# A hybrid decoder layer on one core: the chunk inverse of the delta rule, packed into two 64x64 quarters of the array

## The chip, the core and the metric

The kernel runs on one core of a Trainium2 chip. Its engines are TensorE (PE in the profile; its weight loads are the row PEld), VectorE (DVE), ScalarE (ACT), GpSimd (POOL) and SyncE (SP), which issues most transfers. Each engine takes its own instructions in order and waits on semaphores that others raise. The metric is the device time of one execution in microseconds; less is better.

## The reference, cut to what matters

One layer of a decoder: a norm, one input projection, three groups of heads (sparse attention, Mamba-2, gated DeltaNet), an output projection and an MLP. The change touches the gated DeltaNet scan alone. Per chunk and head it does this:

```python
decay = jnp.exp(jnp.where(incl, cum[..., :, None] - cum[..., None, :], -jnp.inf))
kk = jnp.einsum('bhik,bhjk->bhij', kc, kc)
lower = eye + jnp.where(strict, kk * decay, 0.0) * bc[..., :, None]
rhs = vc * bc[..., None] - jnp.einsum('bhik,bhkv->bhiv', kc * (bc * jnp.exp(cum))[..., None], Sf)
u = lax.linalg.triangular_solve(lower, rhs, left_side=True, lower=True, unit_diagonal=True)
```

`lower` is a unit lower triangular matrix per head, and there are 6 heads of width 128. Everything is float32.

## The kernel before, in words

The work runs in stages: input projection with the sample attention beside it, causal convolutions (`convolve`), the chunk scans (`scans`), the scans' tail, gates and norms, attention with the output projection, and the MLP. Barriers stand between `scans` and its neighbours, so what it saves or loses moves all that follows.

`scans` takes four chunks of 128 tokens (i = 0 to 3) and a tail of 48 tokens (i = 4). Two programs run interleaved on every engine, and `turns()` is the written order in which they alternate. `states()` carries the recurrent states of Mamba-2 ("ssd") and DeltaNet ("gdn") from chunk to chunk. `inverses()` has no recurrence and makes for each chunk the transposed inverse `ttT` of the 6 matrices, one chunk ahead of its use.

`inverses()` for a chunk: PE transposes keys and queries (L1187) and spreads the gates (L1190); DVE and ACT make the decay; PE multiplies keys by keys and queries (L1199); DVE forms the strictly upper triangle `lT` (L1443) and the attention matrix `atT` (L1448). Then the inverse is doubled level by level, from blocks of 1 to blocks of 128: seven levels for a whole chunk, four for the tail. A level k does, for two sets of three heads (x = 0 and 1, one PSUM bank `a_ps[x]` and one `c_ps[x]` each):

- POOL: `mT` = `lT` times a 0/1 mask of the level (L1328), up to two levels ahead, into a ring of two
- PE: `a_ps` = `mT`ᵀ `t` (L1211); ACT copies it into `p1` (L1268)
- PE: `a_ps` = `ttT`ᵀ `p1` (L1217, not at the last level) and `c_ps` = `p1`ᵀ `ttT` (L1220)
- DVE: `ttT` -= `c_ps` (L1467) and `t` -= `a_ps` (L1470)

Level 0 is only identity minus mask: L1457 and L1460. All products are 128x128x128 (48x48x48 in the tail), and a float32 product shows as two records on PE and two on PEld. Lines of `states()` that the text names: L1126 and L1130 (ssd: spread gates, B by C), L1347 (DVE: their differences), L1136, L1363 (DVE: decay by B·C), L1145 and L1149 (ssd: products with the inputs), L1157 (gdn: keys and queries by the state), L1388 to L1398 (DVE: what follows it), L1298 (POOL: `wk`). The turns of a chunk, by PE: L1187, L1190 | state | L1199 | state | level 0, level 1 | state | level 2 | state | level 3 | state | level 4, level 5 | state | level 6. The fourth chunk has fewer state turns.

Of the kernel before, what the change touches and what calls it, by code (L numbers as in the profile page):

```python
# [16 lines left out]
P = 128  # L17
# [1036 lines left out]

def scans(nc, dram, consts, sb):


    with ExitStack() as ctx:
# [24 lines left out]
        mT = lambda k: mT_ring[:, k % 2]  # L1083
# [5 lines left out]
                   "rows_done", "dif", "dec_ready", "decU_ready", "products", "lt_ready", "at_ready", "m_ready")  # L1089
# [7 lines left out]
        lev0 = lambda i: 7 * i  # L1097
        product_ps = lambda c: (a_ps[0], a_ps[1], c_ps[0])[c]
        block = ctx.enter_context(nc.Block())

        @block.sync
        def _(sp):
            sp.dma_start(level[0][:, :], consts["c_level"]).then_inc(p["level_in"], 16)
            sp.dma_start(level[1][:, :], consts["c_level_tail"]).then_inc(p["level_in"], 16)
            sp.wait_ge(p["level_in"], 32)

        @block.tensor
        def _(pe):
# [68 lines left out]
            def inverses():  # L1177
                yield
                for i in range(5):
# [23 lines left out]
                    for lev in range(nlev(i)):  # L1203
                        k = lev0(i) + lev
                        pe.wait_ge(p["m_ready"], k + 1)
                        for x, hs in sets:
                            if lev:
                                pe.wait_ge(t_ready[x], k)
                            for h in range(hs.start, hs.stop):
                                rhs = t[0:n, h, 0:n] if lev else ident[0:n, 0:n]  # L1210
                                last = pe.matmul(a_ps[x][0:n, h % 3, 0:n], mT(k)[0:n, h, 0:n], rhs, start=True, stop=True)  # L1211
                            last.then_inc(p1_done[x], 1)
                        for x, hs in sets if lev else ():
                            pe.wait_ge(p1_out[x], p1_count(i, lev))
                            if lev < nlev(i) - 1:
                                for h in range(hs.start, hs.stop):
                                    pe.matmul(a_ps[x][0:n, h % 3, 0:n], ttT(i)[0:n, h, 0:n], p1[0:n, h, 0:n],  # L1217
                                              start=True, stop=True)
                            for h in range(hs.start, hs.stop):
                                last = pe.matmul(c_ps[x][0:n, h % 3, 0:n], p1[0:n, h, 0:n], ttT(i)[0:n, h, 0:n],  # L1220
                                                 start=True, stop=True)
# [8 lines left out]
        def _(act):  # L1230
# [19 lines left out]
            def inverses():  # L1250
                yield
                for i in range(5):
# [8 lines left out]
                    yield  # L1261
                    yield
                    yield
                    for lev in range(1, nlev(i)):
                        k = lev0(i) + lev
                        for x, hs in sets:
                            act.wait_ge(p1_done[x], k + 1)
                            act.activation(p1[0:n, hs, 0:n], a_ps[x][0:n, 0:3, 0:n], ACT.Copy).then_inc(p1_out[x], 1)  # L1268
# [5 lines left out]
        def _(pool):  # L1274
# [29 lines left out]
            def inverses():  # L1304
                pool.wait_ge(p["level_in"], 32)
                yield
                for i in range(5):
# [12 lines left out]
                    for lev in range(nlev(i)):  # L1320
                        k = lev0(i) + lev
                        for x, _ in sets:
                            if k >= 2:
                                pool.wait_ge(p1_done[x], k - 1)
                            if lev == 2:
                                pool.wait_ge(t_ready[x], k - 1)
                        mask = level[i == 4][0:n, P * lev:P * lev + n]
                        pool.tensor_tensor(mT(k)[0:n, :, 0:n], lT[0:n, :, 0:n], bc(mask.unsqueeze(1), [n, HC, n]), ALU.mult  # L1328
                                           ).then_inc(p["m_ready"], 1)
# [5 lines left out]
        def _(dve):  # L1335
# [83 lines left out]
            def inverses():  # L1419
                yield  # L1420
                scaled_inputs(0)
                for i in range(5):
# [16 lines left out]
                    if i:  # L1439
                        dve.wait_ge(p["m_ready"], lev0(i))  # L1440
# [10 lines left out]
                    yield  # L1451
                    for lev in range(nlev(i)):
                        k = lev0(i) + lev
# [2745 lines left out]
```

## Time and profile before

| | |
|---|---|
| median of 3 runs | 3156.24 us |
| lowest and highest | 3148.05 and 3164.49 us |
| span of the profiled execution | 3150.1 us |
| mean granted clock of TensorE over the span | 0.962 |
| PE busy | 2957.6 us, 94% |
| the four chunks and the tail in `scans`, masks on | 1099.3 to 1332 us |

No device time of the profiled execution stands apart from its span, which lies inside the range of the runs. Times in the rows are microseconds from the span's start. A granted clock of 1.00 is TensorE's 2.4 GHz, 0.50 its 1.2 GHz, and a value between is a share of time at each. "128*128 128x384" is the weights' shape and then what streams; "idle before" in brackets is how long the engine stood and what ended it.

### The profile page before, as it was taken

The page shows a single profiled execution, that of the slowest core. Times are in us where ns is not written, and L with a number is a line of the kernel's source. Part 1 is how long each engine was busy: PE and PEld are TensorE (multiplying, and loading weights), DVE is VectorE, ACT ScalarE, POOL GpSimd, SP SyncE. Part 2 cuts the span into 40 slices and gives each one's busy share as a digit, 9 for nine tenths or more (in the row PEclk, how much of TensorE's full clock was granted, in tenths as well). Part 3 has the DMA queues.
Part 4 walks back from the last instruction along what each step waited for, and adds up shares of the span by engine and source line. Part 5 has one row for each costly group of instructions (what it writes and reads, how often), then busy time and mean ns, then how long its engine had stood idle before and what let it go on. Part 6 is the DMA issues. An engine that isn't in the chain of part 4 may idle for free. (4 is left out here: it accounts for less than half of the span.)

```text
span 3150.1 us, 51111 instructions
## 1 busy us (share of the span) xinstructions
PE 2957.6 (94%) x20787; PEld 2752.5 (87%) x20787; DVE 2360.1 (75%) x3067; ACT 1181.0 (37%) x1736; POOL 667.5 (21%) x477
## 2 busy tenths in 40 slices
PE   7999999999996588887999899999999999999998
PEld 6987898999875487746888899999999999999998
DVE  6149985799543666557985789888988888888887
ACT  4232221222454411134324455555555333333332
POOL 4442333567251143334340000000000000000000
PEclk9999999999997699888999999999999999999999
DMA  5442333569684000048433466666667955565552
GB/s 185 116 141 82 92 102 90 155 214 281 207 256 156 25 1 1 14 128 227 130 108 133 129 187 201 192 184 199 189 194 212 352 180 181 190 205 178 190 171 104
DMA packets 503689, 494.76 MB, mean 157 GB/s; under 512 B 33738, under 2 KB 440618, under 8 KB 501941
## 3 DMA queue, kind: packets, MB, share of 16 engines
q1 hardware_dynamic: 467312, 421.23, 43.9%
q0 software_dynamic: 12928, 42.02, 4.3%
q10 hardware_dynamic: 23216, 28.24, 2.6%
q8 instruction: 166, 2.72, 0.4%
q14 instruction: 67, 0.55, 0.1%
HBM read 378.49 MB, written 114.12 MB: 156 GB/s over the span
## 5 line engine op out<-in xcount | busy, mean ns | idle before, releaser
L3726 PE MATMUL om_ps<-om_hc,om_ring 128*128 128x272 f32 x5376 | 683.3, 290 | 10.6 <-DVE om_ring L3775 6.4
L3726 PEld LDWEIGHTS om_ps<-om_hc,om_ring 128*128 128x128 f32 x5376 | 682.3, 189 | 11.7 <-DVE om_ring L3775 6.8
L3743 PE MATMUL om_ps<-om_hc,om_ring 128*128 128x272 f32 x5376 | 680.8, 290 | 6.6 <-issue 5.1
L3743 PEld LDWEIGHTS om_ps<-om_hc,om_ring 128*128 128x128 f32 x5376 | 679.8, 189 | 7.5 <-issue 6.7
L3962 ACT ACTIVATE om_ring<-om_late 128x1024 fp32r<-128x1024 f32 x301 | 318.7, 1059 | 385.1 <-PE om_ps L3743 263.0
L3775 DVE TENSOR_TENSOR om_ring<-om_late,om_ring 128x1024 fp32r<-128x1024 f32 x301 | 366.1, 1221 | 79.2 <-ACT om_ring L3962 79.0
L565 PE MATMUL pm_ps<-h,w_ring 128*128 128x280 f32 x2688 | 354.9, 293 | 8.4 <-issue 7.8
L565 PEld LDWEIGHTS pm_ps<-h,w_ring 128*128 128x128 f32 x2688 | 348.7, 189 | 14.3 <-issue 14.2
L504 POOL TENSOR_TENSOR w_ring<-w_raw,w_ring 128x1024 fp32r<-128x1024 f32 (+2 forms) x106 | 244.5, 2327 | 340.6 <-ACT w_ring L600 340.4
L3962 ACT ACTIVATE om_ring<-om_raw 128x1024 fp32r<-128x1024 f32 x155 | 164.1, 1059 | 203.2 <-PE om_ps L3743 124.2
L583 PE MATMUL pm_ps<-w_ring,h 128*128 128x512 f32 (+2 forms) x1152 | 237.3, 365 | 2.7 <-PEq L2764 2.7
L583 PEld LDWEIGHTS pm_ps<-w_ring,h 128*128 128x128 f32 x1152 | 199.8, 189 | 36.8 <-issue 3.0
L3775 DVE TENSOR_TENSOR om_ring<-om_raw,om_ring 128x1024 fp32r<-128x1024 f32 x155 | 188.8, 1221 | 50.2 <-ACT om_ring L3962 50.2
L600 ACT ACTIVATE w_ring<-w_raw 128x1024 fp32r<-128x1024 f32 (+2 forms) x124 | 120.8, 1009 | 273.9 <-PE as_dead_bank L583 187.4
L3893 DVE TENSOR_TENSOR om_x<-om_x,om_ps 128x544 f32<-128x544 f32 x224 | 160.6, 717 | 79.0 <-PE om_ps L3743 76.8
L2269 PE MATMUL ao_w<-ao_mh,ao_ring 128*128 128x272 f32 x1152 | 180.0, 308 | 2.2 <-DVE ao_mh L2460 2.2
L2269 PEld LDWEIGHTS ao_w<-ao_mh,ao_ring 128*128 128x128 f32 x1152 | 155.8, 192 | 18.6 <-issue 12.5
L632 ACT ACTIVATE pm_stage<-pm_ps 128x280 f32<-128x280 f32 (+3 forms) x64 | 29.1, 455 | 179.0 <-PE pm_ps L565 133.7
L3278 DVE TENSOR_TENSOR as_prod<-as_rows,as_qb 128x512 f32<-128x512 f32 x64 | 95.7, 1495 | 0.0
L3159 POOL DMA_INDIRECT as_rows<-in_cache_v,as_offs x64 | 71.8, 1122 | 89.1 <-PE as_o_bank L3425 75.0
L565 PEld LDWEIGHTS pi_ps<-h,w_ring 128*128 128x128 f32 x672 | 86.4, 188 | 0.9 <-issue 0.8
L565 PE MATMUL pi_ps<-h,w_ring 128*128 128x280 f32 x672 | 86.9, 291 | 0.0
(614 smaller groups left out, 4111.6 us busy)
## 6 DMA issues: line engine op xcount, KB each, us to landing
hid_scratch<-om_x SPq DMA_DIRECT2D x64, 952.0 KB, 7.4
om_hc<-hid_scratch SPq DMA_DIRECT2D x56, 1088.0 KB, 11.7
w_raw<-in_w_in SPq DMA_DIRECT2D x112, 512.0 KB, 4.2
om_late<-in_w_up SPq DMA_DIRECT2D x85, 512.0 KB, 5.0
om_late<-in_w_down SPq DMA_DIRECT2D x85, 512.0 KB, 5.2
om_raw<-in_w_up SPq DMA_DIRECT2D x43, 512.0 KB, 4.8
om_raw<-in_w_down SPq DMA_DIRECT2D x43, 512.0 KB, 5.0
ao_raw<-in_w_out SPq DMA_DIRECT2D x32, 384.0 KB, 3.9
```

Source lines behind the costliest of these rows:

```text
L504: eng.tensor_tensor(f32r(ring[:, n % 2, 1, half_of(q, n)]), raw[:, q, whole(q, n)], ring[:, n % 2, 0, half_of(q, n)], ALU.subtract).then_i ...
L565: ins = pe.matmul(bank_of(b + y)[:, 0:HALF], piece(a, k), f32r(h[:, x, k, two_halves(y)]), start=first, stop=last)
L583: ins = pe.matmul(bank_of(b + m)[:, 0:w], f32r(h[:, x, ld.k0 + k, tok]), piece(a, k), start=first, stop=last)
L600: act.activation(f32r(ring[:, n % 2, 0, half_of(q, n)]), raw[:, q, whole(q, n)], ACT.Copy).then_inc(hi_ready[q], 1)
L2269: ins = pe.matmul(w_ps[2 * (n % 2) + half][:, 0:HM], w, f32r(mh[:, b, k, kept_half(half)]), start=first, stop=last)
L3159: pool.indirect_dma_start(self.rows[:, n % RING, :], None, table, bass.IndirectOffsetOnAxis(ap=self.offs[:, x, j:j + 1], axis=0)).then_inc ...
L3278: dve.tensor_tensor(prod[:, n % 2, :], self.rows[:, n % RING, :], self.qb[:, j % 4, :], ALU.mult).then_inc(s["multiplied"], 1)
L3726: last = pe.matmul(ps[:, bank_of(q, idx), 0:HM], f32r(ring[:, n % SLOTS, a, P * k:P * (k + 1)]), f32r(hc[:, c, b, k, :]), start=(idx in (0 ...
L3743: last = pe.matmul(ps[:, bank_of(q, idx) + i, 0:HM], w, f32r(hc[:, slot, b, GJ * half + j, :]), start=(idx in (0, 1, 3) and j == a == b == 0),
L3775: dve.tensor_tensor(f32r(ring[:, n % SLOTS, 1, :]), source(n), ring[:, n % SLOTS, 0, :], ALU.subtract).then_inc(lo, 1)
L3893: dve.tensor_tensor(dst, dst, ps[:, b:b + 2, 0:HM], ALU.add).then_inc(gathered, 1)
L3962: act.activation(f32r(ring[:, n % SLOTS, 0, :]), source(n), ACT.Copy).then_inc(hi, 1)
```

## The change

For whole chunks the first six levels, in which all is block diagonal with two blocks of 64, keep only the two blocks, one above the other: `t`, `p1`, the new `tt` and `lp`, and the masks' ring hold 64 columns a head in place of 128. A product of 128x128x128 becomes two of 64x64x64, one with both operands and its result in partitions 0 to 63, one in 64 to 127, issued in turn into the same bank. The last level is one off-diagonal block: two products of 64x64x64 a head, and DVE writes it negated. ACT makes a packed copy `lp` of `lT` from which POOL takes the masks of levels 1 to 5; level 0 takes them from `lT` in two halves; the mask of level 6 is gone. The tail keeps its shapes. The level table is loaded as 6x64 columns in two transfers. Buffers shrink with it, and an `eye` and two zeroed blocks are written once.

```diff
+HB2 = P // 2
+PACKED = 6
+BLOCKS = (slice(0, HB2), slice(HB2, P))
...
-        level = [sbuf("level", [P, 7 * P]), sbuf("level_tail", [P, 4 * P])]
-        lT, t, p1, dec, decU, beta_upto = (sbuf(n, [P, HC, P]) for n in ("lT", "t", "p1", "dec", "decU", "beta_upto"))
-        mT_ring = sbuf("mT", [P, 2, HC, P])
+        level, level_tail = sbuf("level", [P, PACKED, HB2]), sbuf("level_tail", [P, 4 * P])
+        lT, dec, decU, beta_upto = (sbuf(n, [P, HC, P]) for n in ("lT", "dec", "decU", "beta_upto"))
+        lp, t, p1, tt = (sbuf(n, [P, HC, HB2]) for n in ("lp", "t", "p1", "tt"))
+        mT_ring = sbuf("mT", [P, 2, HC, HB2])
...
                             for h in range(hs.start, hs.stop):
-                                rhs = t[0:n, h, 0:n] if lev else ident[0:n, 0:n]
-                                last = pe.matmul(a_ps[x][0:n, h % 3, 0:n], mT(k)[0:n, h, 0:n], rhs, start=True, stop=True)
+                                if join:
+                                    last = pe.matmul(a_ps[x][BLOCKS[1], h % 3, 0:HB2], lT[BLOCKS[0], h, BLOCKS[1]],
+                                                     t[BLOCKS[0], h, :], start=True, stop=True)
+                                    continue
+                                for b in blocks_of(i):
+                                    w = b.stop - b.start
+                                    rhs = t[b, h, 0:w] if lev else eye[b, 0:w]
+                                    last = pe.matmul(a_ps[x][b, h % 3, 0:w], mT(m)[b, h, 0:w], rhs, start=True, stop=True)
...
                                 for h in range(hs.start, hs.stop):
-                                    pe.matmul(a_ps[x][0:n, h % 3, 0:n], ttT(i)[0:n, h, 0:n], p1[0:n, h, 0:n],
-                                              start=True, stop=True)
+                                    for b in blocks_of(i)[0:1] if lev == PACKED - 1 else blocks_of(i):
+                                        w = b.stop - b.start
+                                        pe.matmul(a_ps[x][b, h % 3, 0:w], tt[b, h, 0:w], p1[b, h, 0:w], start=True, stop=True)
...
+                    if i < 4:
+                        act.wait_ge(p["lt_ready"], i + 1)
+                        if i:
+                            act.wait_ge(p["m_ready"], masks_before(i))
+                        for b in BLOCKS:
+                            act.activation(lp[b, :, :], lT[b, :, b], ACT.Copy).then_inc(p["lp_ready"], 1)
...
-                            act.activation(p1[0:n, hs, 0:n], a_ps[x][0:n, 0:3, 0:n], ACT.Copy).then_inc(p1_out[x], 1)
+                            act.activation(p1[b, hs, 0:w], a_ps[x][b, 0:3, 0:w], ACT.Copy).then_inc(p1_out[x], 1)
...
+                        elif lev == 0:
+                            for b in BLOCKS:
+                                last = pool.tensor_tensor(mT(m)[b, :, :], lT[b, :, b],
+                                                          bc(level[b, lev, :].unsqueeze(1), [HB2, HC, HB2]), ALU.mult)
+                            last.then_inc(p["m_ready"], 1)
+                            pool.wait_ge(p["m_ready"], m + 1)
+                        else:
+                            pool.wait_ge(p["lp_ready"], 2 * (i + 1))
+                            pool.tensor_tensor(mT(m), lp[:, :, :], bc(level[:, lev, :].unsqueeze(1), [P, HC, HB2]), ALU.mult
+                                               ).then_inc(p["m_ready"], 1)
...
+                            if i < 4 and lev == PACKED:
+                                last = dve.tensor_scalar(ttT(i)[BLOCKS[0], hs, BLOCKS[1]], c_ps[x][BLOCKS[0], 0:3, 0:HB2], -1.0,
+                                                         None, ALU.mult)
+                            elif i < 4 and lev == PACKED - 1:
+                                for b in BLOCKS:
+                                    dve.tensor_tensor(ttT(i)[b, hs, b], tt[b, hs, :], c_ps[x][b, 0:3, 0:HB2], ALU.subtract)
+                                b = BLOCKS[0]
+                                last = dve.tensor_tensor(t[b, hs, :], t[b, hs, :], a_ps[x][b, 0:3, 0:HB2], ALU.subtract)
...
+                            else:
+                                dve.tensor_tensor(tt[0:n, hs, 0:w], tt[0:n, hs, 0:w], c_ps[x][0:n, 0:3, 0:w], ALU.subtract)
+                                last = dve.tensor_tensor(t[0:n, hs, 0:w], t[0:n, hs, 0:w], a_ps[x][0:n, 0:3, 0:w],
                                                          ALU.subtract)
```

The order on PE, from level 5 of the first chunk to the transposes of the second. First before (columns: line, operation, result and operands, shape, count):

```order
L1211 MATMUL sc_a<-sc_t,sc_mT 128x128 x6
L1217 MATMUL sc_a<-sc_p,sc_ttT 128x128 x3
L1220 MATMUL sc_c<-sc_ttT,sc_p 128x128 x3
L1217 MATMUL sc_a<-sc_p,sc_ttT 128x128 x3
L1220 MATMUL sc_c<-sc_ttT,sc_p 128x128 x3
L1157 MATMUL sc_e<-st,sc_kq 128x128 x12
L1211 MATMUL sc_a<-sc_t,sc_mT 128x128 x6
L1220 MATMUL sc_c<-sc_ttT,sc_p 128x128 x6
L1187 MATMUL sc_a<-ident,tm 128x128 x12
```

Then the same place in the changed kernel:

```order
L1240 MATMUL sc_a<-sc_t,sc_mT 64x64 x12
L1254 MATMUL sc_a<-sc_p,sc_tt 64x64 x3
L1258 MATMUL sc_c<-sc_tt,sc_p 64x64 x6
L1254 MATMUL sc_a<-sc_p,sc_tt 64x64 x3
L1258 MATMUL sc_c<-sc_tt,sc_p 64x64 x6
L1176 MATMUL sc_e<-st,sc_kq 128x128 x12
L1234 MATMUL sc_a<-sc_t,sc_lT 64x64 x6
L1246 MATMUL sc_c<-sc_ttT,sc_p 64x64 x6
L1206 MATMUL sc_a<-ident,tm 128x128 x12
```

Nothing has changed places: each group of three heads is twice as many products of an eighth of the size each, the product into `a_ps` at level 5 is made for the upper block alone, and level 6 has one product a head in each of its two steps.

On GpSimd the masks of a chunk, before (the second chunk, from `decU` on):

```order
L1316 TENSOR_TENSOR sc_decU<-sc_dec,sc_beta_upto 128x768
L1328 TENSOR_TENSOR sc_mT<-sc_lT,sc_level 128x768
L1328 TENSOR_TENSOR sc_mT<-sc_lT,sc_level 128x768
L1283 TENSOR_TENSOR sc_xdt<-tm,dt 128x768
L1285 TENSOR_TENSOR sc_skip<-tm,ssm_d 128x768
```

and in the changed kernel:

```order
L1362 TENSOR_TENSOR sc_decU<-sc_dec,sc_beta_upto 128x768
L1382 TENSOR_TENSOR sc_mT<-sc_lT,sc_level 64x384
L1382 TENSOR_TENSOR sc_mT<-sc_lT,sc_level 64x384
L1388 TENSOR_TENSOR sc_mT<-sc_lp,sc_level 128x384
L1329 TENSOR_TENSOR sc_xdt<-tm,dt 128x768
```

The mask of level 0 has become two operations of half the partitions and half the columns, and that of level 1 one of half the columns, which waits for ACT's copy.

## Rows read from the trace of the kernel before

**Rows 1.** The page: busy time, share of the span and instructions of each engine.

```profile
PE 2957.6 (94%) x20787; PEld 2752.5 (87%) x20787; DVE 2360.1 (75%) x3067; ACT 1181.0 (37%) x1736; POOL 667.5 (21%) x477
```

**Rows 2.** Windows: stretch, length, PE, PEld, DVE, ACT, POOL busy, PEclk, DMA, GB/s.

```profile
1217.50:1275.50 58.00, 50.50 (x374) 45.75 (x373) 38.01 (x75) 10.12 (x19) 22.95 (x13) 0.94 0.00 1
```

**Rows 3.** Timeline of one inverse level with no other work between.

```profile
1302.71 0.91 PE L1211 MATMUL sc_a<-sc_t,sc_mT 128*128 128x128 f32 x6
...
1303.66 0.49 ACT L1268 ACTIVATE sc_p<-sc_a 128x384 f32<-128x384 f32 x1 [3.03 <-PE sc_a L1211]
...
1304.73 0.83 PE L1217 MATMUL sc_a<-sc_p,sc_ttT 128*128 128x128 f32 x6
...
1305.40 0.83 PE L1220 MATMUL sc_c<-sc_ttT,sc_p 128*128 128x128 f32 x6
...
1306.35 0.56 DVE L1467 TENSOR_TENSOR sc_ttT<-sc_ttT,sc_c 128x384 f32<-128x384 f32 x1 [2.44 <-PE sc_c L1220]
...
1307.51 0.68 PE L1211 MATMUL sc_a<-sc_t,sc_mT 128*128 128x128 f32 x4
```

**Rows 4.** Timeline of the third chunk: what its queues wait for.

```profile
1219.48 1.57 PE L1211 MATMUL sc_a<-ident,sc_mT 128*128 128x128 f32 x12 [0.49 <-POOL sc_mT L1328]
1220.21 1.72 DVE L1457 TENSOR_TENSOR sc_ttT<-ident,sc_mT 128x768 f32<-128x768 f32 x1
...
1222.66 1.57 PE L1211 MATMUL sc_a<-sc_t,sc_mT 128*128 128x128 f32 x12 [1.60 <-DVE sc_t L1460]
...
1226.93 2.84 PE L1126 MATMUL sc_e<-upto,g 128*128 128x128 f32 x24
...
1238.06 3.90 DVE L1363 TENSOR_TENSOR sc_sdec<-sc_sdec,sc_gm 128x768 f32<-128x768 f32 x2
...
1242.22 3.38 PE L1145 MATMUL sc_e<-sc_xdt,sc_sdec 128*128 128x64 f32 x24 [2.32 <-DVE sc_sdec L1363]
...
1247.94 1.50 PE L1211 MATMUL sc_a<-sc_t,sc_mT 128*128 128x128 f32 x12
...
1252.23 0.91 PE L1211 MATMUL sc_a<-sc_t,sc_mT 128*128 128x128 f32 x6
...
1256.93 2.84 PE L1157 MATMUL sc_e<-st,sc_kq 128*128 128x128 f32 x24
...
1264.78 3.50 PE L1187 MATMUL sc_a<-ident,tm 128*128 128x128 f32 x12 [2.15 <-DVE sc_ttT L1467]
```

**Rows 5.** Timeline: L1363 in the first chunk, GpSimd idle.

```profile
1094.10 2.17 DVE L1363 TENSOR_TENSOR sc_sdec<-sc_sdec,sc_gm 128x768 f32<-128x768 f32 x2 [1.26 <-ACT sc_sdec L1236]
```

**Rows 6.** Timeline of the tail: products of 48x48, and a change of size.

```profile
1319.00 1.63 PEld L1170 LDWEIGHTS sc_e<-sc_u,sc_wk 128*128 128x128 f32 x12 [0.25 <-issue]
...
1325.13 0.35 PEld L1220 LDWEIGHTS sc_c<-ttT_tail,sc_p 48*48 48x48 f32 x6
...
1327.09 0.28 ACT L1268 ACTIVATE sc_p<-sc_a 48x144 f32<-48x144 f32 x1 [2.00 <-PE sc_a L1211]
...
1328.73 0.29 DVE L1467 TENSOR_TENSOR ttT_tail<-ttT_tail,sc_c 48x144 f32<-48x144 f32 x1 [1.96 <-PE sc_c L1220]
...
1388.30 1.39 PEld L1669 LDWEIGHTS tl_e<-tl_xdt,tl_sdec 48*48 48x48 f32 x24 [0.21 <-issue]
```

**Rows 7.** GpSimd's masks, by tile sc_lT: minimum/median/maximum ns.

```profile
L1328 POOL TENSOR_TENSOR sc_mT<-sc_lT,sc_level x28: 1796/1813/2238, 1099.3 to 1300.2; 128x768 f32<-128x768 f32 x28
L1328 POOL TENSOR_TENSOR sc_mT<-sc_lT,sc_level_tail x4: 786/794/805, 1319.8 to 1325.0; 48x288 f32<-48x288 f32 x4
```

**Rows 8.** The same columns as rows 2, in stretches of two us.

```profile
1245.50:1247.50 2.00, 2.00 (x5) 1.09 (x5) 1.23 (x3) 0.00 (x0) 0.00 (x0) 0.50 0.00 0
1324.00:1326.00 2.00, 1.84 (x36) 1.74 (x36) 0.41 (x3) 0.55 (x2) 1.54 (x2) 1.00 0.00 0
1328.00:1330.00 2.00, 2.00 (x26) 1.90 (x24) 0.82 (x4) 0.00 (x0) 0.00 (x0) 0.50 0.00 0
1376.00:1378.00 2.00, 2.00 (x7) 0.74 (x6) 0.09 (x1) 1.86 (x2) 0.05 (x1) 1.00 0.90 343
```

More of the change, by code:

```diff
@@ L1102, in _ @@
         def _(sp):
[L1103 to L1105 removed]
+            by_level = consts["c_level"].rearrange("p (l c) -> p l c", c=P)
+            for b in BLOCKS:
+                sp.dma_start(level[b, :, :], by_level[b, 0:PACKED, b]).then_inc(p["level_in"], 16)
+            sp.dma_start(level_tail[:, :], consts["c_level_tail"]).then_inc(p["level_in"], 16)
+            sp.wait_ge(p["level_in"], 48)
         @block.tensor
@@ L1203, in inverses @@
                     for lev in range(nlev(i)):
-                        k = lev0(i) + lev
-                        pe.wait_ge(p["m_ready"], k + 1)
+                        k, m = lev0(i) + lev, masks_before(i) + lev
+                        join = i < 4 and lev == PACKED
+                        if not join:
+                            pe.wait_ge(p["m_ready"], m + 1)
+                        if k == 0:
+                            pe.wait_ge(p["eye_ready"], 2)
                         for x, hs in sets:
@@ L1214, in inverses @@
                             pe.wait_ge(p1_out[x], p1_count(i, lev))
+                            if join:
+                                for h in range(hs.start, hs.stop):
+                                    last = pe.matmul(c_ps[x][BLOCKS[0], h % 3, 0:HB2], p1[BLOCKS[1], h, :],
+                                                     ttT(i)[BLOCKS[1], h, BLOCKS[1]], start=True, stop=True)
+                                last.then_inc(q_done[x], 1)
+                                continue
                             if lev < nlev(i) - 1:
                                 for h in range(hs.start, hs.stop):
-                                    pe.matmul(a_ps[x][0:n, h % 3, 0:n], ttT(i)[0:n, h, 0:n], p1[0:n, h, 0:n],
-                                              start=True, stop=True)
+                                    for b in blocks_of(i)[0:1] if lev == PACKED - 1 else blocks_of(i):
+                                        w = b.stop - b.start
+                                        pe.matmul(a_ps[x][b, h % 3, 0:w], tt[b, h, 0:w], p1[b, h, 0:w], start=True, stop=True)
                             for h in range(hs.start, hs.stop):
-                                last = pe.matmul(c_ps[x][0:n, h % 3, 0:n], p1[0:n, h, 0:n], ttT(i)[0:n, h, 0:n],
-                                                 start=True, stop=True)
+                                for b in blocks_of(i):
+                                    w = b.stop - b.start
+                                    last = pe.matmul(c_ps[x][b, h % 3, 0:w], p1[b, h, 0:w], tt[b, h, 0:w],
+                                                     start=True, stop=True)
                             last.then_inc(q_done[x], 1)
@@ L1304, in inverses @@
             def inverses():
[L1305 removed]
+                pool.wait_ge(p["level_in"], 48)
                 yield
@@ L1419, in inverses @@
             def inverses():
+                for b in BLOCKS:
+                    dve.tensor_copy(eye[b, :], sb["ident"][b, b]).then_inc(p["eye_ready"], 1)
+                for n in range(2):
+                    dve.memset(ttT_ring[BLOCKS[1], n, :, BLOCKS[0]], 0.0).then_inc(p["eye_ready"], 1)
+                dve.wait_ge(p["eye_ready"], 4)
                 yield
@@ L1439, in inverses @@
                     if i:
-                        dve.wait_ge(p["m_ready"], lev0(i))
+                        dve.wait_ge(p["m_ready"], masks_before(i))
+                        dve.wait_ge(p["lp_ready"], 2 * i)
+                        for x, _ in sets:
+                            dve.wait_ge(p1_done[x], lev0(i))
                     for c in range(3):
```

47 lines of the change are left out of this document (30 added, 17 removed).

## Prediction

> **What bounds the kernel now.** I read the page first: PE is busy for 94% of the span [rows 1], but the change touches only the scans, so the stretch decides and not the share. The windows cut the scans into periods. From one chunk's level 0 to the next it is 58 us, with PE busy for 50.5, DVE for 38.0, ACT for 10.1 and GpSimd for 23.0, at a mean granted clock of 0.94 [rows 2]. The timeline of a period says which wait ends last where [rows 4]. PE waits four times: for the mask of level 0 (0.49 us), for DVE's first `t` (1.60), for DVE's decay products L1363 before L1145 (2.32), and for DVE's last `ttT` before the transposes (2.15). Between these it runs without a gap. So the period is a chain that passes from PE to DVE and back, and a faster PE alone gains only where PE carries it.
>
> A level with nothing between shows the chain itself [rows 3]: 4.80 us from L1211 to L1211. The first group of three heads is 6 records; its end is seen by ACT 0.95 us after its start (1302.71 to 1303.66), ACT copies in 0.49, two further groups a set take 0.67 each (L1217 at 1304.73, L1220 at 1305.40), DVE starts 0.28 after the latter and PE 1.16 after DVE. A group of 6 records passes in 0.67 us, 111 ns a record.
>
> **The change, part by part.**
>
> *PE's products.* A group of 6 records becomes 12 of 64 columns. The nearest row for one: 24 records of 48 weights and 64 streamed columns in the tail of the scans take 1.39 us, 57 ns each, all in one quarter [rows 6]. If the two quarters do not overlap, a group is 12 x 57 = 0.68 us against 0.67: nothing gained. If they overlap fully, 0.34. No row shows two quarters at work at once, so both ends stay open. The fastest issue that a row shows is no help: six loads of 48 columns within 0.35 us, under 58 ns each, and 2 x 48 columns at 2.4 GHz are 40 of these, the stream and not the issue [rows 6]. I take 0.35 for a group in the overlapped case.
> The Trainium skill ("TensorE: Matmul & The Clock Gate", Part 3) states that products in different row and column tiles run side by side with starts some 4 ns apart; by it the group costs 0.34 us. No row here shows it.
>
> *DVE and ACT.* 384 columns cost DVE 0.55 to 0.56 us and 144 cost 0.29; ACT 0.49 and 0.28 [rows 3, 6]. For 192 columns I take 0.35 and 0.32. That is 0.2 less for each of four DVE operations a level and 0.17 for a copy on the chain. L1457 at level 0, 1.72 us for 768 columns, halves to 0.86. Level 5 has three DVE operations a set in place of two and stays even; level 6 is 0.35 against 0.55.
>
> *GpSimd.* 288 columns take 0.79 us, 768 take 1.81 [rows 7]; 384 then take 1.0. Level 0 needs two of them, 2.0 against 1.81, and PE waits for this mask: 0.2 lost a chunk. The others are halved and lie under PE's levels. L1363 takes 3.90 us in the third chunk, where `wk` (L1298) runs on GpSimd beside it [rows 4], and 2.17 in the first, with GpSimd idle [rows 5]. In the changed order `wk` stands in the same place but starts when level 3's first product ends, so its overlap may shrink or not: 0 to 1.7 us gained, and I take 0.3.
>
> *Costed at nothing.* ACT's two `lp` copies (64x384, about 0.5 each by the 0.49 for 384 columns) start when `lT` is ready; ACT's next work is level 1's `p1`, some 6 us later, and the level 1 mask that waits for them is issued behind 2.0 us of level 0 masks. Without that cover they would cost 1.0 a chunk. The `eye` copies, the zero writes (under 1.5 us together at 0.35 each) and the narrower level table (128 x 6 pieces of 256 bytes) come before the first mask by 15 us or more and are under the scan's first gates.
>
> *Change of size.* Behind products of 48 weight columns, PE stands 0.25 us before the first full-width load of L1170 [rows 6]. A chunk now has ten such changes, five blocks of small products. Three lie on the chain (level 1 to L1126, L1149 to level 4, level 5 to L1157); 3 x 0.2 = 0.6 a chunk.
> "TensorEngine Tiling (Array Packing)", Key Properties, in the Trainium skill says that changing the mode drains the engine; the row agrees with a drain of about this size.
>
> *The sum if quarters overlap and the clock stays.* Third chunk, from [rows 4]: level 0, from 1219.48 to 1222.66: 0.86 and 0.2 less on DVE, 1.06. Level 1, 1222.66 to 1226.93 = 4.27, becomes 0.35 + 0.3 + 0.32 + 0.25 + 4 x 0.35 = 2.6: 1.6. Level 2 falls under DVE's queue, which now leads: four updates x 0.2 = 0.8, and L1363 0.3. Level 4: 4.8 becomes (0.35 + 0.3 + 0.32 + 0.3 + 0.7 + 0.28 + 0.76) = 3.0; in this chunk it was 4.3 (1247.94 to 1252.23), since both sets were ready, so 1.3. Level 5, 1252.23 to 1256.93 = 4.7, becomes 2.6: 2.1. Level 6 is hidden under DVE's four us of L1388 to L1398; its two updates give 0.4. Less 0.2 for the mask and 0.6 for the changes of size: 1.06 + 1.6 + 0.8 + 0.3 + 1.3 + 2.1 + 0.4 - 0.8 = 6.8. Three such periods: 20. The fourth chunk has four levels of 4.4 to 4.8 in a row or nearly: 1.1 at level 0, 1.5 at each of levels 1, 4 and 5, 1.3 + 0.4 around levels 2 and 3, 2.2 at level 6, less 0.6: about 9. Together 29 us.
>
> *The clock.* This is where I choose against that sum. In the tail, whose products are all 48x48, the granted clock is 1.00 at 1324 and 0.50 at 1328 to 1330, though PE is busy for all of those two us [rows 8]. In the chunks it fell to 0.50 only after PE had stood (1245.5, behind the wait for L1363) [rows 8]. Yet weights of 48 columns streaming 384 columns held 1.00 at 1376, with PE busy throughout [rows 8]. The packed levels lie between: 64x64, two at once, with PE standing longer for DVE than now (4 to 5 us before L1145). So part of the levels should run at 1.2 GHz. There an overlapped group costs 6 x 111 = 0.67, as now, and the full-width work behind it is slower until the clock returns: L1126 and L1130 (3.1 us) and L1157 (2.7) could each double, and L1145 lose 1. If all of it is at half clock, a chunk keeps the 1.06 of level 0, 0.3 for each of levels 4 and 5, about 0.4 at level 2 and 0.4 at level 6, less 0.8: 1.7 gained against 6.8 lost, 5 slower; three of these and nothing in the fourth make 15 us. I take the middle of 29 gained and 15 lost, 7 to 10 gained, as neither end has a row that decides: 9.
> The same first page of the skill, Part 1, says that the clock follows how busy the engine is; by it the sum of 29 would stand. The tail's row disagrees.
>
> The sum is made on an execution of 3150.1 us span, 0.2% below the median, and is taken from the median: 3156.2 - 9 = 3147.
>
> **The rivals.**
>
> *Overlap at full clock:* the 29 us, less if a record pair takes nearer 90 ns than 58 (then about 20). 3126 to 3137, middle 3130. For it: the row at 1376. Against: the rows at 1328.
>
> *No overlap, full clock:* both quarters write one bank, `a_ps[x]` or `c_ps[x]`; if their results or loads queue, PE's group stays at 0.68. What is left is level 0 (1.06), 0.2 at level 2, 0.9 at level 5 (its `a_ps` product is half), 0.4 at level 6, less 0.2 and 0.6 to 0.8: 1.8 a chunk, three times, and 4 in the fourth, where level 6's 24 records replace 24 of twice the length: 9 to 10 gained. 3147. It would give my time for another reason.
> The skill's "TensorEngine Tiling (Array Packing)", Gotcha 1, says that different row tiles cannot use one PSUM bank at the same time; by it this is the case.
>
> *Slower, the clock:* overlap, but nearly every level and what follows at 1.2 GHz: 15 lost, 3171. It decides against the change from the point where 29/44, two thirds, of this part of the scans are at half clock.
>
> *Slower, both:* no overlap and half clock: 72 records of 111 ns are 8.0 us a level against 4.0; four levels, 1.3 at level 0 and 2.7 at level 5 make 20 a chunk, 15 to 20 of it uncovered, and the 6.8 above: 85 to 105 us, 3250.
>
> **How the numbers follow.** Part of the levels at half clock, my forecast, 0.35, from 3136 to 3160. Overlap at full clock 0.27. No overlap at full clock 0.13. Nearly all at half clock 0.13. Both 0.08. The remaining 0.04 is a cost that I do not see. A difference within 0.5%, 15.8 us, is about what a measurement of this kernel cannot tell from no change. Faster by more than that, under 3140.5: nearly all of the second case and a quarter of the first, 0.33. Slower, over 3172: the last two and under half of the fourth, 0.19. Within: 0.48. The range leaves out the last two cases and the far end of the second: 3124 to 3172.
>
> **What would show it.** After: a level with nothing between of 3.0 us, a group of 12 weight loads within 0.35 to 0.4 us (overlap) or 0.68 (none); PE standing 4 us or more before L1164, as L1145 is then called; the granted clock of a chunk's period 0.7 to 0.85 (my case), 0.9 or more (the fast one), 0.6 (the slow one); periods of 51 (fast), 55 to 57 (mine) or over 60 us. The prediction is wrong if the clock holds, or if the quarters queue and the clock falls.

## The result and the profile after

The changed kernel takes 3117.19 us (median of 4 runs, 3116.68 to 3122.01), the kernel before on the same chip 3152.88. The ratio is 0.9889 with a 95% interval of 0.9861 to 0.9917: 1.1% faster, 36 us by the medians. The prediction was 3147, with a range of 3124 to 3172. The result lies below the range; the gain is nearer to the 29 us that the prediction had summed and then discounted than to the 9 that it forecast.

The page of the profiled execution (span 3115.0 us), the line that answers to [rows 1]:

```profile
PE 2917.8 (94%) x21507; PEld 2709.4 (87%) x21507; DVE 2337.9 (75%) x3079; ACT 1178.1 (38%) x1744; POOL 656.6 (21%) x477
```

PE is busy for 40 us less and keeps as large a share of a shorter span. Windows of the same columns as [rows 2], from one chunk's level 0 to the next; the third row takes in the 48 tokens of the tail and ends at the first product of the next stage:

```profile
1145.80:1194.10 48.30, 40.27 (x554) 34.74 (x554) 32.21 (x77) 9.25 (x21) 19.86 (x14) 0.93 0.01 2
1194.10:1244.50 50.40, 42.73 (x552) 36.72 (x552) 32.12 (x77) 9.25 (x21) 19.72 (x14) 0.86 0.01 1
1244.50:1295.20 50.70, 40.18 (x600) 36.88 (x601) 24.29 (x68) 7.72 (x24) 11.62 (x13) 0.79 0.01 2
```

Periods of 58.0 us have become 48.3 and 50.4. PE is busy for 40 to 43 us instead of 50.5, DVE for 32 instead of 38. The granted clock is 0.93 and 0.86, against 0.94.

The timeline of the second chunk, which [rows 3, 4] show for before:

```profile
1145.88 0.92 PE L1240 MATMUL sc_a<-sc_eye,sc_mT 64*64 64x64 f32 x24 [0.73 <-POOL sc_mT L1382]
1146.37 0.86 DVE L1526 TENSOR_TENSOR sc_tt<-sc_eye,sc_mT 128x384 f32<-128x384 f32 x1
...
1147.77 0.92 PE L1240 MATMUL sc_a<-sc_t,sc_mT 64*64 64x64 f32 x24 [0.97 <-DVE sc_t L1529]
...
1149.85 0.52 PE L1258 MATMUL sc_c<-sc_tt,sc_p 64*64 64x64 f32 x12
...
1150.30 2.94 PE L1145 MATMUL sc_e<-upto,g 128*128 128x128 f32 x24
...
1154.61 0.56 PE L1254 MATMUL sc_a<-sc_p,sc_tt 64*64 64x64 f32 x12
1155.01 0.52 PE L1258 MATMUL sc_c<-sc_tt,sc_p 64*64 64x64 f32 x12
1155.36 0.52 PE L1254 MATMUL sc_a<-sc_p,sc_tt 64*64 64x64 f32 x12
...
1160.34 4.05 POOL L1344 TENSOR_TENSOR sc_wk<-tm,wend 128x768 f32<-128x768 f32 x1
1160.38 1.81 DVE L1423 TENSOR_TENSOR sc_sdec<-sc_sdec,sc_gm 128x768 f32<-128x768 f32 x2
...
1162.44 3.54 PE L1164 MATMUL sc_e<-sc_xdt,sc_sdec 128*128 128x64 f32 x24 [1.82 <-DVE sc_sdec L1423]
...
1168.25 0.91 PE L1240 MATMUL sc_a<-sc_t,sc_mT 64*64 64x64 f32 x24
...
1171.04 1.17 PE L1240 MATMUL sc_a<-sc_t,sc_mT 64*64 64x64 f32 x24 [0.18 <-DVE sc_t L1549]
...
1173.56 2.94 PE L1176 MATMUL sc_e<-st,sc_kq 128*128 128x128 f32 x24
...
1181.10 0.73 PE L1206 MATMUL sc_a<-ident,tm 128*128 128x128 f32 x4 [2.78 <-DVE sc_ttT L1537]
...
1194.08 0.92 PE L1240 MATMUL sc_a<-sc_eye,sc_mT 64*64 64x64 f32 x24 [0.72 <-POOL sc_mT L1382]
```

A group of 12 loads starts 0.35 us before the next (1155.01, 1155.36), 29 ns a load; the six loads of the same group before passed in 0.67. The table goes from start to start. The column "before" is the third chunk of [rows 4], with its next level 0 one period of [rows 2] later; the last column has the terms of the prediction's sum.

| from PE's start of | to | before | after | gained | in the prediction |
|---|---|---|---|---|---|
| level 0 | level 1 | 3.18 | 1.89 | 1.29 | 1.06 |
| level 1 | L1145 | 4.27 | 2.53 | 1.74 | 1.6 - 0.2 |
| L1145 | level 4 | 21.01 | 17.95 | 3.06 | 0.8 + 0.3 - 0.2 |
| level 4 | level 5 | 4.29 | 2.79 | 1.50 | 1.3 |
| level 5 | L1176 | 4.70 | 2.52 | 2.18 | 2.1 - 0.2 |
| L1176 | transposes L1206 | 7.85 | 7.54 | 0.31 | 0.4 |
| transposes | next level 0 | 12.7 | 12.98 | -0.3 | -0.2 |
| sum | | 58.0 | 48.20 | 9.8 | 6.8 |

The third chunk repeats these rows but for three stretches in which the clock is low: 18.66, 3.37 and 13.95 us in place of 17.95, 2.79 and 12.98. That is 2.3 us, and its gain is 7.6. The first chunk gained 7.4. From the fourth chunk's level 0 to the first product of the next stage 6.0 were gained: 8.7 in the chunk itself (34.5 us before, 25.8 after), less 2.7 in the tail of 48 tokens, whose work on PE did not change. It begins here:

```profile
1270.31 2.22 PE L1206 MATMUL sc_a<-ident,tm 48*128 48x48 f32 x12 [0.56 <-issue]
```

From 1270.3 to 1280.3 the granted clock is 0.50, with PE busy for 9.74 us; before, it was 0.83 in the tail's first 10 us.

I measure the inverse part of the scans from the first transposes to the first product of the next stage (`tl_e`), since the work ahead starts at times that differ from run to run (below). Two rows of before, two of after:

```profile
1083.98 1.12 PE L1187 MATMUL sc_a<-ident,tm 128*128 128x128 f32 x4 [5.64 <-DVE tm L1417]
...
1334.19 1.05 PE L1640 MATMUL tl_e<-upto,g 48*128 48x48 f32 x4 [2.14 <-PEq L2579]
```

```profile
1075.68 3.53 PE L1206 MATMUL sc_a<-ident,tm 128*128 128x128 f32 x12 [5.71 <-DVE tm L1477]
...
1295.21 1.05 PE L1719 MATMUL tl_e<-upto,g 48*128 48x48 f32 x4 [2.19 <-PEq L2658]
```

This stage takes 250.2 us before and 219.5 after: 30.7 gained. The stage began 8.3 us earlier in the changed kernel's profile, and later stages gave 3.9 back; together that is the 35.1 between the spans. The 8.3 cannot be put down to the change: in the twelve other profiles below the stage starts between 1075.7 and 1082.9 us, at 1080.1 in the one of the kernel before, although none of them edits anything ahead of it. For the 3.9 no run shows a cause.

### The profile page after: what moved, and what is told of

It reads as the page before. It is cut to its first block and busy times, and to the rows that moved or that the text cites. A ratio compares the mean times of both kernels' runs of the same rounds, so it can differ in the third digit from the quotient of the medians.

```text
span 3115.0 us, 52579 instructions
## 1 busy us (share of the span) xinstructions
PE 2917.8 (94%) x21507; PEld 2709.4 (87%) x21507; DVE 2337.9 (75%) x3079; ACT 1178.1 (38%) x1744; POOL 656.6 (21%) x477
```

## Experiments

"Stage" is the stretch just defined, 219.5 us in the changed kernel and 217.7 in a second profile of it, so a difference of 2 us between two stages says nothing. Where a kernel ran several times the median of its runs stands beside the stage; "one run" is a single time.

### Does the overlap carry the gain, or the halved copies?

**Upper block issued twice.** In the three loops over `blocks_of(i)`:

```
-for b in blocks_of(i):
+for b in (BLOCKS[:1] if i < 4 else ()) + tuple(blocks_of(i)):
```

> The upper block's products are issued twice, so that a group is 12 loads in one quarter and 6 in the other, 0.68 us instead of 0.35, what a group would cost if the quarters took turns; the outputs stay. Theory A (the gain comes half from two products side by side, and PE leads in levels 1, 4, 5 and at the ends of the others): an isolated level goes from 2.8 to about 3.8 us, the stage grows by 4 to 6 us a chunk, 219.5 to 235 to 243, the kernel near 3135 to 3140, so that half or more of the gain is the overlap. Theory B (DVE's and ACT's halved operations carry the gain, PE has slack): the stage grows by under 8 us. Should the granted clock fall with it, the transposes and L1145, L1176 show it.

Timeline of levels 4 and 5, PE, and the window of the chunks:

```profile
1181.63 1.61 PE L1240 MATMUL sc_a<-sc_t,sc_mT 64*64 64x64 f32 x36
...
1183.07 0.86 PE L1254 MATMUL sc_a<-sc_p,sc_tt 64*64 64x64 f32 x18
1183.77 0.86 PE L1258 MATMUL sc_c<-sc_tt,sc_p 64*64 64x64 f32 x18
...
1185.87 1.86 PE L1240 MATMUL sc_a<-sc_t,sc_mT 64*64 64x64 f32 x36
```

```profile
1080.00:1290.00 210.00, 187.29 (x2736) 167.78 (x2735) 126.35 (x275) 35.71 (x78) 63.83 (x49) 0.92 0.01 2
```

A group takes 0.70 us and a level 4.24 instead of 2.79. The stage is 245.8 us, 26.2 more, and the kernel 3146.72 us (10 runs; ratio to before 0.9986, 0.9966 to 1.0007). With DVE, ACT and GpSimd still on half the columns, 26 of the 31 us are gone. Theory A holds and more strongly than it said: the gain is two products side by side, and the other halved operations are worth it only behind a faster PE. The clock does not explain the loss: it is 0.92 here, 0.91 in the same window before and 0.87 in the changed kernel. This is nearly the prediction's rival without overlap, but costs somewhat more: the first group of level 5 has 12 loads in one quarter here, and the rival has 6.

**DVE's updates doubled.** Each update of levels 1 to 4 is also written to a spare tile:

```
+if i < 4:
+    dve.tensor_tensor(junk[:, 2*x], tt[:, hs, :], c_ps[x][:, 0:3, 0:w], ALU.subtract)
+    dve.tensor_tensor(junk[:, 2*x+1], t[:, hs, :], a_ps[x][:, 0:3, 0:w], ALU.subtract)
```

> The changed kernel, with each of DVE's two updates of a set at levels 1 to 4 done once more into an unused buffer ahead of the real one: 8 more operations of about 0.27 us spacing in a level pair of sets, 1.1 us of DVE a level, about what the halving took from it (0.8). If the periods are now led by DVE, as the forecast had it, the stage grows by 3 to 4.4 us a chunk, 12 to 17 in all. If PE leads, by under 5.

```profile
1171.11 4.87 PE L1164 MATMUL sc_e<-sc_xdt,sc_sdec 128*128 128x64 f32 x24 [2.57 <-DVE sc_sdec L1423]
```

The stage is 230.5 us, 11.0 more (one run 3133.77). The wait for L1423 is 2.57 us in place of 1.82. The wait for `t` before the fourth chunk's level 4 is 3.38 in place of 2.85. So both engines stand on the chain. The 11 us lie just under the 12 at which the expectation has DVE lead throughout, and not all of them are DVE's: in the fourth chunk the clock fell during level 4 and stayed down.

```profile
1277.50:1288.00 10.50, 9.03 (x118) 7.96 (x115) 5.09 (x16) 1.31 (x4) 0.00 (x0) 0.50 0.01 2
```

### What do the quarters need in order to overlap?

**Block by block.** All of a group's upper products, then all of its lower ones:

```
-for h in range(hs.start, hs.stop):
-    for b in blocks_of(i):
+for b in blocks_of(i):
+    for h in range(hs.start, hs.stop):
```

> The changed kernel, with the products of a group of three heads issued block by block: three heads of the upper 64 rows, then three of the lower, in place of upper and lower in turn. Same products, same results. I measure the scans from the first transposes to the first product of the stage behind: 250.2 us before, 220.0 us changed (1075.7 to 1295.6). Theory A, the gain comes from two quarters working at once, and this needs neighbouring products in different quarters: a group of 12 weight loads goes from 0.35 us to 0.6 or 0.7, the stage to 235 to 243 us, the whole to about 3137. Theory B, the gain comes from the halved work of DVE, ACT and GpSimd: the group is longer but the stage stays under 225. On the clock: if it is two quarters at once that keeps it at 2.4 GHz, the granted clock of the chunks falls clearly below the 0.9 of the changed kernel; if any busy PE does, it stays.

```profile
1203.08 1.08 PE L1240 MATMUL sc_a<-sc_t,sc_mT 64*64 64x64 f32 x24
1204.23 0.61 PE L1254 MATMUL sc_a<-sc_p,sc_tt 64*64 64x64 f32 x10
1204.63 0.22 PE L1258 MATMUL sc_c<-sc_tt,sc_p 64*64 64x64 f32 x1
```

The expected loss did not come. The stage is 222.1 us, the median 3121.46 (4 runs; ratio 0.9910, 0.9886 to 0.9935). L1258's first record starts among L1254's last: the upper quarter goes on to the next group while the lower one still works, so the pace of 0.35 us a group stays, and only a level's first product is longer (1.08 against 0.92). So the edit did not take the overlap away, and only the doubled issue above says what the overlap is worth.

**Both blocks from the same rows.** Weights and streamed data of the lower block's products are taken from rows 0 to 63 (`o = BLOCKS[0]`), the results still go to rows 64 to 127; the lower block's inverse is not computed.

> The changed kernel, with the lower block's products of levels 0 to 5 reading the upper block's operands (partitions 0 to 63) and writing the lower half as now: two quarters that share their rows and differ in columns. The lower block's inverse is left out, the upper one's is there twice. Theory 1, two quarters overlap only if their rows differ too: a group of 12 loads takes 0.6 to 0.7 us and the stage 235 us or more. Theory 2, different columns are enough: 0.35 us and 220.

The pace is again 0.35 us a group: distinct columns of the array are enough. But the stage is 231.8 us, 12.2 more (one run 3129.6), which nothing in the expectation covers. Windows show it:

```profile
1168.00:1186.00 18.00, 17.85 (x169) 15.86 (x169) 8.93 (x20) 1.32 (x4) 3.77 (x2) 0.50 0.00 1
```

PE is busy for 17.85 of 18 us and the granted clock stands at 0.50 throughout, through L1164, L1168 and levels 4 and 5. In the changed kernel's whole chunks no stretch at 0.50 is longer than 7 us (1212.2 to 1219.0).

### Why does the clock hold in the changed kernel?

Its own fourth chunk is the first answer. Timeline and two-us windows:

```profile
1260.08 1.55 PE L1240 MATMUL sc_a<-sc_t,sc_mT 64*64 64x64 f32 x24 [2.85 <-DVE sc_t L1549]
1261.40 0.91 PE L1254 MATMUL sc_a<-sc_p,sc_tt 64*64 64x64 f32 x12
...
1263.38 0.54 PE L1258 MATMUL sc_c<-sc_tt,sc_p 64*64 64x64 f32 x12
```

```profile
1260.00:1262.00 2.00, 1.93 (x36) 1.96 (x37) 0.46 (x2) 0.66 (x2) 0.00 (x0) 0.50 0.00 0
1264.00:1266.00 2.00, 1.68 (x46) 1.55 (x44) 0.62 (x2) 0.66 (x2) 0.00 (x0) 1.00 0.00 0
1290.00:1292.00 2.00, 1.82 (x23) 1.66 (x22) 0.72 (x3) 0.31 (x2) 0.00 (x0) 0.50 0.00 0
```

After a wait of 2.85 us the level starts at half clock, 1.2 GHz, a group every 0.64 to 0.70 us. Nothing but pairs of 64x64 runs, and by 1263.4 the clock is back at 2.4 GHz. In the second profile of the same kernel it takes from 1258.5 to 1264.5. The tail's 48x48 products, in one quarter, are at half clock at 1290, as they were at 1328 before [rows 8].

Pairs do not always bring it back. In the run with DVE's updates doubled the clock is 0.50 from 1277.5 to 1288.0: 6.5 us with pairs, then level 6, whose products stand alone, PE busy for 9.03 of the 10.5 us. It is the only such stretch. In the nine profiles in which both blocks work in opposite quarters, no other stretch at 0.50 in the whole chunks is longer than 7 us. The three others (same rows, above, and the two that follow) have eight of 10 us or more; the longest are 20.5, 20.5 and 27.3 us.

**One block only.** From level 2 of the first chunk on, and in every level of the later chunks, the lower block's products are left out, so its inverse is not computed:

```
-for b in blocks_of(i):
+for b in (blocks_of(i) if lev0(i) + lev < 2 else blocks_of(i)[0:1]):
```

> From the third level on the lower block's products are left out (its inverse is not computed); the upper block's 6 loads of 64 columns take the 0.35 us that 12 loads in two quarters took, everything else is as in the changed kernel. Theory A (pace): 57 ns a load in one quarter, so PE is as long busy and the stage stays within 3 us of 219.5. Theory C (the granted clock follows how much of the array works, as it seemed when both blocks used the same rows and the stage grew by 12 us with stretches of 16 us at half clock): the granted clock stands at 0.50 over long stretches of the chunks, and the stage grows by 15 us or more. If the clock holds, the 12 us of the shared rows have another cause.

```profile
1080.00:1290.00 210.00, 179.41 (x1415) 157.36 (x1415) 120.61 (x277) 35.10 (x78) 70.86 (x49) 0.74 0.00 1
1174.00:1192.00 18.00, 17.80 (x124) 15.55 (x123) 6.55 (x17) 1.97 (x6) 0.00 (x0) 0.56 0.00 1
1177.80:1186.00 8.20, 8.06 (x73) 7.83 (x72) 3.25 (x9) 1.32 (x4) 0.00 (x0) 0.50 0.01 2
```

At full clock its 6 loads take the 0.35 us of a pair's 12, so PE's work is as long. Yet the stage is 244.6 us, 25.1 more (one run 3144.75), and the mean granted clock 0.74 against 0.87. From 1174 to 1192 PE is busy for 17.80 of 18 us at 0.56; levels 4 and 5 in it, one quarter and nothing else, for 8.06 of 8.20 us at 0.50. What theory C forecast came true; pace alone would have left 219.5.

**One block, issued twice.** As the last, with `* 2` on the upper block: 12 loads in one quarter.

> From the third level on the lower block's products are left out, and the upper block's are issued twice: 12 loads in one quarter, 0.70 us a group, as long as in the run with 12 loads in one quarter and 6 in the other (stage 245.8 us, granted clock 0.92 from 1080 to 1290 us). The two differ only in the 6 loads of the lower quarter. Theory C (the clock falls and stays low where only one quarter works, however busy TensorE is): the granted clock over the chunks is 0.75 to 0.85, as the 0.74 with one block issued once, and the stage is 255 us or more. Theory D (the clock fell in the one-block run for its gaps, not for its quarter): TensorE is busy for longer here, the clock stays at 0.9 or more, and the stage is within 3 us of 245.8.

```profile
1080.00:1290.00 210.00, 187.18 (x1909) 167.81 (x1910) 118.44 (x261) 34.76 (x75) 63.40 (x48) 0.85 0.01 1
```

```profile
1234.77 5.35 PE L1164 MATMUL sc_e<-sc_xdt,sc_sdec 128*128 128x64 f32 x24 [1.57 <-DVE sc_sdec L1423]
1239.92 2.87 PE L1168 MATMUL sc_e<-sc_xdtw,tm 128*128 128x384 f32 x4
1242.72 2.82 PE L1240 MATMUL sc_a<-sc_t,sc_mT 64*64 64x64 f32 x24
1245.34 1.49 PE L1254 MATMUL sc_a<-sc_p,sc_tt 64*64 64x64 f32 x12
```

The stage is 257.0 us (one run 3154.33), 11.2 more than with 12 and 6 loads, the clock 0.85 against 0.92; PE is busy for 187 us in both. But 9.0 of the 11.2 are one period, the third chunk's, 67.1 us against 58.1, and this is one profile. There the clock fell behind the wait for L1423 and stood at 0.50 from 1234.2 to 1261.5, levels 4 and 5 included: PE busy for 15.50 of 15.50 us (2.82 and 1.49 us in the rows). In the second chunk it had fallen in the same place and was back at 1183, just as level 4 began, and the same levels then ran at 1.00, PE busy for 8.62 of 8.70 us. So theory C was too simple. Work in one quarter kept a full clock here. In four stretches of 8 us or more, this one and three of the run with one block, it did not bring a fallen one back, where pairs mostly did; twice in the run with one block the clock was back within 1 us of level 4's start, behind L1164 and L1168. Which part the full-width work between has in this is open, and so is what else decides it.

### What waits now, and can it be shortened?

**GpSimd's `wk` late, in the kernel before.** GpSimd waits for L1363 before it starts `wk`:

```
+if i < 3:
+    pool.wait_ge(s["w_ready"], i + 2)
```

> The kernel before, with GpSimd's wk (L1298) of the first three chunks made to wait until DVE's decay products L1363 are done. In the changed kernel L1363 takes 1.8 us against 3.9, with wk starting later than it. If that comes from wk alone, L1363 takes 1.8 to 2.2 here and each of three periods shortens by about 2: the stage from 250.2 to 244 to 245. Rival: L1363 is slow for another reason, or what follows (L1368, then beside wk) takes it back: 249 to 250.

```profile
1228.27 1.81 POOL L1330 TENSOR_TENSOR sc_mT<-sc_lT,sc_level 128x768 f32<-128x768 f32 x1 [3.67 <-PE sc_a L1211]
1229.14 2.63 DVE L1365 TENSOR_TENSOR sc_sdec<-sc_sdec,sc_gm 128x768 f32<-128x768 f32 x2
```

L1363 (here L1365) takes 2.63 us instead of 3.90, the stage 245.7 instead of 250.2 (one run 3142.64). What is left over the 1.8 below is the mask beside it.

**Scaling later.** `scaled_inputs(i + 1)` behind level 4, where DVE idles, instead of level 2:

```
-if i < 4 and lev == 2:
+if i < 4 and lev == 4:
```

> The scaling of the next chunk's queries and keys on DVE (L1477, 1.75 us) is issued after level 4 instead of after level 2. Theory A (in a period of the changed kernel DVE's queue between level 2 and the decay products L1423 sets when PE's L1164 may start; PE stands 1.82 us for L1423): the wait before L1164 almost goes, 1.5 to 1.8 us less in each of the three whole periods, the stage from the first transposes to the tail's first product 219.5 to about 214 to 215 us, and the kernel 5 us, 0.15%, faster than the changed kernel, near 3112. Theory B (PE's packed products set the period, DVE only follows): under 1 us. Should the scaling now be late for the next transposes, the wait before L1206 grows by the same amount and nothing is gained.

**Scaling later, `wk` late.** With the wait of the run on the kernel before.

> As the scaling moved behind level 4, and GpSimd's wk (L1344) also waits until the decay products of the same stretch (L1423) are done. If the two engines slow each other there, L1423 falls from about 1.8 to 1.1 or 1.2 us for the pair and PE's L1164 starts 0.6 us earlier a period: 1 to 2 us below the run with the scaling alone, about 3110. If wk comes too late for L1189, or the next chunk's beta products behind it in GpSimd's queue do, PE waits there and the time is equal or above.

The first gives a stage of 216.3 us and a median of 3115.05, the second 210.9 and 3113.99 (6 runs each, ratios 0.9873 and 0.9880). The wait for L1423 was expected to go almost wholly. It stayed at 1.31 us in both, and the timeline of the second says why:

```profile
1153.97 2.62 DVE L1425 TENSOR_TENSOR sc_sdec<-sc_sdec,sc_gm 128x768 f32<-128x768 f32 x2
1153.99 1.79 POOL L1390 TENSOR_TENSOR sc_mT<-sc_lp,sc_level 128x384 f32<-128x384 f32 x1 [3.40 <-PE sc_a L1240]
...
1156.84 3.23 PE L1164 MATMUL sc_e<-sc_xdt,sc_sdec 128*128 128x64 f32 x24 [1.31 <-DVE sc_sdec L1425]
```

Moved forward by 1.75 us, L1423 (here L1425) meets level 5's mask on GpSimd, and both are slowed: 2.62 and 1.79 us against 1.81 and 0.99. Each is longer by 0.8, about one of L1423's two operations (0.9), as if each had waited once for the other; no run tests this.

**Level 5's mask late as well.**

```
+if lev == 5 and i < 3:
+    pool.wait_ge(s["w_ready"], i + 2)
```

> With the scaling moved behind level 4, DVE's decay products L1423 started at once but took 2.62 us for the pair, beside GpSimd's level 5 mask, which took 1.79 us in place of 0.99. Here that mask also waits until L1423 is done, then wk. Theory A (the two engines slow each other, and L1423 still decides when PE's L1164 may start): L1423 falls to 1.1 to 1.2 us for the pair, the wait before L1164 goes, the period falls from 47.9 to about 46.5 us, the stage from 216 to 211 to 212, the kernel to about 3109. Theory B (L1423 is slow for another reason, or the mask is late for level 5): the pair stays near 2.6 us, or PE waits for the mask before level 5, and the time stays at 3114 or more.

```profile
1157.20 1.82 DVE L1427 TENSOR_TENSOR sc_sdec<-sc_sdec,sc_gm 128x768 f32<-128x768 f32 x2
...
1159.28 2.86 PE L1164 MATMUL sc_e<-sc_xdt,sc_sdec 128*128 128x64 f32 x24 [0.51 <-DVE sc_sdec L1427]
...
1161.98 1.51 PE L1168 MATMUL sc_e<-sc_xdtw,tm 128*128 128x384 f32 x4
```

L1423 (L1427) is at 1.82, not at the 1.1 that I took for its floor; the wait is 0.51 us, and behind it L1164 and L1168 keep the full clock, 2.86 and 1.51 us where the changed kernel has 3.54 and 2.54. That is the larger part. The periods from level 0 to level 0 are 46.2, 45.2 and 46.4 us, the stage 206.7. The median is 3108.75 us (6 runs, 3103.72 to 3117.61; ratio 0.9855, 0.9830 to 0.9880).

**The waits alone, and the changed kernel again.**

> The changed kernel with its scaling where it was, and only the two waits on GpSimd: level 5's mask and wk start when the decay products L1423 are done. Theory A: L1423 falls from 1.8 to 1.1 or 1.2 us and the wait before L1164 from 1.82 to 1.2, 0.6 to 0.7 us a period, 2 us in all: near 3115, not to be told from the changed kernel. Theory B: no change of L1423, and the masks or wk late for PE: above 3117.

> The changed kernel once more, on the same chip as the two others, to set them against it: 3117 us within 0.2%.

```profile
1161.57 1.82 DVE L1427 TENSOR_TENSOR sc_sdec<-sc_sdec,sc_gm 128x768 f32<-128x768 f32 x2
...
1163.65 4.33 PE L1164 MATMUL sc_e<-sc_xdt,sc_sdec 128*128 128x64 f32 x24 [1.83 <-DVE sc_sdec L1427]
```

With only the waits L1423 stays at 1.82 us and PE's wait at 1.83: in the changed kernel L1423 was not slowed at all, and `wk`, started 0.04 us ahead of it, bore the whole delay (4.05 us). The median is 3116.61 us. The changed kernel again gives a stage of 217.7 us, with periods of 50.6, 51.6 and 48.2 where the first profile has 50.7, 48.2 and 50.5: the short one is that in which the clock fell least. Its median is 3116.19 (6 runs, 3113.69 to 3119.65; ratio 0.9879, 0.9856 to 0.9902). The version with all three edits is thus 7.4 us, 0.24%, under it by the medians. The two intervals overlap, so a gain is likely and not settled. Against the kernel before its whole interval lies at 1.2 to 1.7% faster.

## Why the prediction was wrong

**The sum of 29 us** came out: the stage gained 30.7. Levels 1, 4 and 5 came out at 2.53, 2.79 and 2.52 us, where 2.6, 3.0 and 2.6 were estimated. The group at 0.35 us, the operations of 192 columns at 0.35 (DVE) and 0.33 (ACT, with two in 0.68), L1457 halved to 0.86, the half-size masks at 0.99: each was right. That the total is so near is in part luck. The second chunk gained 9.8 and not 6.8, three times that is 9 us more than summed, and the clock took 7 back.

**The overlap** was left open between 0.68 and 0.34 us a group, and is 0.35. Here the Trainium skill's "TensorE: Matmul & The Clock Gate", Part 3, is right that products in different tiles run side by side. "TensorEngine Tiling (Array Packing)", Gotcha 1, in the Trainium skill is not borne out: the two quarters are in different rows and columns, write one bank, `a_ps[x]` or `c_ps[x]`, and still pass 12 loads in 0.35 us.

**The step that failed is the clock.** "So part of the levels should run at 1.2 GHz", and then "I take the middle of 29 gained and 15 lost": that took 20 us off a sum that was right (the middle would be 7, and 9 was taken). The inference went from the tail's 48x48 products, one quarter at work, to pairs of 64x64. The runs separate the two for the most part. Pairs brought the clock back after a wait in the changed kernel's fourth chunk and in its repeat, and did not in 6.5 us of the run with DVE doubled; one quarter did not bring it back (one block: 0.74 in the window of the chunks; one block twice, 27 us at 0.50). By the row at 1328 of [rows 8] one quarter was the suspect as much as the size; I had no row for a pair, and the middle of two ends was a choice, not a reading. The clock did fall behind waits. Against the second chunk that cost 2.4 us in the first and 2.3 in the third, and 2.7 in the tail: a price of about 7 where I put 20. "TensorE: Matmul & The Clock Gate" in the Trainium skill says in Part 1 that the clock follows how busy the engine is. By it the sum of 29 would have stood; the one-block run, busy for 17.80 of 18 us at 0.56, disagrees with it. What the clock follows beyond this is open.

**L1363** was the term most mis-sized: 0.3 taken, 2.1 a chunk measured (3.90 to 1.81), outside the stated 0 to 1.7. The prediction had `wk` start later. It starts beside L1423, but bears the delay itself, and the mask, now short, is done before both. This is 1.8 of the 3.0 us by which the second chunk beat its sum.

**The changes of size** were put at 0.2 each. L1145 starts 0.45 us after the last group of level 1 (1149.85 to 1150.30), where another group would have started after 0.35, so 0.1. The extra wait for level 0's mask is 0.73 against 0.49: 0.2, as taken. PE did not stand 4 to 5 us before L1164 but 1.82. "PE waits four times" was a misreading that cost nothing: in the same period it also waits 0.34 us for `t` within level 5 and 0.49 for DVE before L1199.

**The rivals.** Full overlap at full clock, 3126 to 3137, was nearest and still 9 us too slow. The 29 us taken from 3156.2 give 3127, 10 above the measured time: about 2 of these are the stage, 4 lie outside it in the two profiled executions, and 3 are the base, whose median was 3152.88 with the fourth run. Without overlap, the prediction gave 9 to 10 us gained. With it imposed, 4.5 were left in the stage and 7 by the medians, with a little more work than the rival had. That 3146.72 stands beside the rival's 3147 is closer than this, because the kernel before was at 3153.53 in that comparison.

## What to carry to other kernels

Two independent 64x64 products in opposite quarters pass at the pace of one, and the pace, not the halved copies, was the gain; it is kept here even when they are issued block by block. When a sum from rows is sound and a single doubt without a row would take most of it away, keep the sum as the forecast and put the doubt in the range. After PE is shortened, look for the DVE operation that it now waits for and for what GpSimd does at that moment: moving the operation forward gave little (3115.05) until the GpSimd work beside it was moved too (3108.75), and there the shorter wait was repaid twice, in the wait and in the clock behind it.

## What the runs showed of the hardware that I had not expected

- Two quarters run ahead of each other: with the blocks issued in turn, the records of neighbouring groups interleave and the pace stays at 29 ns a load. Sharing the rows does not change the pace either.
- The granted clock depends on more than PE's busy time. One quarter at work, PE busy for 8.06 of 8.20 us, stood at 0.50; both blocks out of the same rows, with the full-width work ahead of them 17.85 of 18, at 0.50. Pairs in opposite quarters went back to 1.00 within 3.3 and 6.0 us of the end of a wait, and once did not in 6.5. The same one-quarter levels ran at 1.00 in one chunk and at 0.50 in the next, PE busy throughout in both.
- Which of two engines pays when they work beside each other is not fixed: L1423 beside a mask 2.62 us and the mask 1.79 (alone 1.82 and 0.99); beside a `wk` that started 0.04 us before it 1.81, and `wk` 4.05 in place of 2.05 to 2.18.
